# Modulation chunks of the latent attention: column tiles of 32, five chunks together in each pair of heads, one turn for all

## The chip, the cores and the metric

The kernel runs on one core of a Trainium2 chip, as one launch. The metric is the device time of that launch in microseconds (us), the median of several runs; less is better. The engines are TensorE (PE in the rows; PEld is its weight load), VectorE (DVE), ScalarE (ACT), GpSimd (POOL), and SyncE (SP), whose queue here only issues transfers.

## What is computed

One step of a two-layer diffusion model on 128 prompt tokens and 512 sample tokens, in float32. Each layer has a mixer (layer 0: latent attention; layer 1: retention) and a mixture of experts, and both are modulated by vectors that come from a condition:

```python
def modulation(cond, w, b):
    m = jax.nn.silu(cond) @ w + b
    return jnp.split(m, 6, axis=-1)
...
mod_c = modulation(cond_ctx, ada_w[layer], ada_b[layer])
mod_l = modulation(c, ada_w[layer], ada_b[layer])
hc = modulate(xc, norm1_g[layer], mod_c[0], mod_c[1])
...
oc, ctx_kv = mla_context(hc, ...)          # layer 0: 8 heads, keys and values from a latent
ol = mla_latent(hl, cache_mla[:, j], ...)  # 512 queries over 512 + 128 keys
xc = xc + mod_c[2][:, None, :] * oc
```

There are two conditions (one for the prompt, one for the sample), so each modulation is a product of 2 rows of 1024 with a matrix of 1024 x 6144, for two layers: 24 chunks of 512 columns in all.

## The kernel before

**Stages.** `setup` transposes the input and makes `silu_cond`, the two conditions after silu as [128, 8, 2]. Then, for layer 0, `mla_project` (norm, down-projections), `mla_pairs` (attention, four pairs of heads in a loop), the experts; then layer 1. The change touches `setup`, `mla_project` and `mla_pairs`. Engines meet at the end of each stage's block; within a block each engine runs its own list of instructions, and waits on semaphores that the others raise. The order in each list is written out by hand.

**Chunks.** A chunk of `ada_w` is [1024, 512], 2 MB, in one of the slots of a ring of weights. `ada_chunk` multiplies it as the moving operand: eight products over k, with the two columns of `silu_cond` as weights. Product k writes to partitions 32*(k%4) and the one after it, so four stand side by side in the array's columns, at partitions 0, 32, 64 and 96 of one PSUM bank. Each float32 product is two matmuls in the trace. The result is 2 useful rows in each of four groups. DVE copies the bank to SBUF (`take_rows`, L876 in the pairs, L532 in `mla_project`), PE turns it (`ada_turn`, L283: four products with `pick`, which adds the four groups and leaves 2 columns each), and DVE adds the bias into `modulation` (L882, L541). Four chunks (`FIRST`) are done in `mla_project`, five (`PER_PAIR`) in each of the four pairs.

**A pair of heads.** In the order of PE's list: q (three products), keys, S0 and S1, values v0 to v2, then ten units u, one for each of 2 heads x 5 tiles of 128 queries. S(u) are the scores of unit u (L706 and L707; over 640 keys, but over 128 for u = 0 and 5). DVE takes their maximum (L901, L899), ACT the exponential, DVE divides (L859), PE transposes (T(u), L716), and ACT and DVE copy the transposed tile out (L814, L865). PE issues S(u+2) ahead of T(u). After T8 and T9 come O0 and O1, the products with the values, and then w0 to w7, the output projection (L801). The chunks A0 to A4 and their turns B0 to B2 stand between these: A0, A1 ahead of S2; B0 after T1; A2 ahead of T4; B1 after T5; A3 ahead of T8; A4 after O1; B2 ahead of w2. Bank n of a product is given by its place in the list `order` modulo 4, and the helper `free` makes PE wait for whoever empties what stood four places earlier.

**DVE's list** in unit u: maximum of S(u), then the division for u-1, then the copy of T(u-1), then what `TAKE_AT` and `BIAS_AT` ask for. So a copy of a chunk's rows stands ahead of the maximum of the next unit.

**Transfers.** SP loads the next pair's chunk x into its slot once the product `A{x}` of this pair is done.

Of the kernel before, what the change touches and what calls it, by code (L numbers as in the profile page):

```python
# [20 lines left out]
P = 128  # L21
D = 1024
KD = D // P
# [51 lines left out]
BASE_COLS = {"ident": P, "ones": P, "before": P, "iota16": NE, "iota4": NG, "iotab": NBLK, "pick": 2}  # L75
# [17 lines left out]
def shape_constants():  # L93
# [5 lines left out]
            one * np.arange(NBLK), p % 32 == np.arange(2)]  # L99
# [64 lines left out]
def setup(c, cond):  # L164

    nc, ops, ps = c.nc, c.ops, c.ps
    with ExitStack() as st:
# [7 lines left out]
        with nc.Block(no_gpsimd_drain=True) as block:  # L175
# [15 lines left out]
            @block.gpsimd  # L191
            def _(pool):
                pool.memset(c.eps[:, :], EPS).then_inc(memsets, 1)
                pool.memset(rows_b[:, :], 0.0).then_inc(memsets, 1)

            @block.scalar
            def _(act):
# [3 lines left out]
                act.wait_ge(memsets, 2)  # L201
# [14 lines left out]
                for j in range(2):  # L216
                    nc.scalar.activation(cond[:, :, j], c.cols_b[:, 8 * j:8 * j + 8], ACT.Silu).then_inc(silued, 1)

            @block.tensor
            def _(pe):  # L220
                pe.wait_ge(consts_in, 16)
                pe.wait_ge(rows_in, 16 * 7)
                pe.wait_ge(memsets, 2)
# [162 lines left out]
def mla_project(c, m, j, call, amp, shift):  # L386
# [5 lines left out]
    with ExitStack() as st:  # L392
# [6 lines left out]
        ada_rows = sq[:, :, :].rearrange("p b n -> p (b n)")[:, 0:FIRST * 512].rearrange("p (x n) -> p x n", x=FIRST)  # L399
        cleared, ada_used, ada_rowed, ada_turned, biased = sems(  # L400
            nc, st, "ada", ["cleared", "used", "rows", "turned", "biased"])
# [13 lines left out]
        with nc.Block(no_gpsimd_drain=True) as block:  # L415
# [22 lines left out]
            def _(pe):  # L438
                def first_chunk(n):
                    pe.wait_ge(c.ada_first[n], 16)  # L440
                    ada_chunk(c, pe, n, (0, 3, 4, 5)[n]).then_inc(ada_used, 1)

                def first_turn(n):
                    pe.wait_ge(ada_rowed, n + 1)
                    ada_turn(c, pe, ps[:, 4, 8 * n:8 * n + 8], ada_rows[:, n, :]).then_inc(ada_turned, 1)

                pe.wait_ge(cleared, 1)
# [5 lines left out]
                for n in range(FIRST):  # L453
                    first_turn(n)
# [74 lines left out]
            def _(dve):  # L529
                def take_rows(n):  # L530
                    dve.wait_ge(ada_used, n + 1)
                    dve.tensor_copy(ada_rows[:, n, :], ps[:, n, :]).then_inc(ada_rowed, 1)  # L532
# [8 lines left out]
                dve.tensor_tensor(c.mod[:, 0, 0:16, :], ps[:, 4, 0:32].rearrange("p (m j) -> p m j", j=2),  # L541
                                  c.cols_a[:, 32:48].unsqueeze(2).to_broadcast([P, 16, 2]), ALU.add).then_inc(biased, 1)
# [64 lines left out]
def mla_pairs(c, m, layer, j):  # L607
# [5 lines left out]
    TURNS = ((0, 1), (2,), (3, 4))  # L613
    ADA_AT, TURN_AT, TAKE_AT, BIAS_AT = {4: 2, 8: 3}, {1: 0, 5: 1}, {1: (0, 1), 4: (2,), 8: (3,)}, {3: 0, 6: 1}
    order = ["q0", "q1", "qp", "k0", "qs", "k1", "S0", "S1", "v0", "v1", "v2", "A0", "A1"]
    for u in range(NU):
        order += ([f"S{u + 2}"] if u + 2 < NU else []) + ([f"A{ADA_AT[u]}"] if u in ADA_AT else []) + [f"T{u}"]
        order += ([f"B{TURN_AT[u]}"] if u in TURN_AT else []) + (["O0"] if u == NU - 2 else [])
    order += ["O1", "A4"] + [f"w{d}" for d in range(KD)]
# [1534 lines left out]
```

## Time and profile before

| | |
|---|---|
| time, median of 3 runs | 2346.25 us (2345.98 to 2348.88) |
| the profiled execution | 2346.19 us |
| its span, first to last instruction | 2344.5 us |
| PE busy | 2086.2 us, 89% of the span |
| DVE busy | 1151.9 us, 49% |
| ACT busy | 897.7 us, 38% |
| mean granted clock of TensorE | 0.908 of full |

The profiled execution took 1.69 us more than its span. The share of an engine is the union of its instructions' times; PE's 89% is no measure of how well it is used, since the four products of a chunk that run side by side count once. The row PEclk gives the clock that TensorE was granted in tenths of 2.4 GHz; the chip knows two levels, 2.4 and 1.2 GHz. A digit between 5 and 9 is a mean over a slice in which both occurred.

### The profile page before, as it was taken

Reading aid. Unit: us, or ns where it says so; the run is one execution under the profiler, and the core shown is the slowest. Engines: PE = TensorE matmul, PEld = TensorE weight load, DVE = VectorE, ACT = ScalarE, POOL = GpSimd, SP = SyncE. Lnnn points to the kernel's source line nnn. Section 1 sums busy time; section 2 is a strip of 40 time slices with the busy share of each in tenths; the row PEclk is TensorE's granted clock in tenths of the full one; section 3 lists DMA queues with packets and bytes.
Section 4 is the critical chain, followed back from the end, with each engine's and each line's share of the span. In section 5 each row is a group of like instructions: output and inputs, shape, how many; then the busy total and the mean of one; then the engine's idle time right before and its main releaser. Section 6 shows DMA issues by size and latency. Waiting matters only on the chain. (4 is left out here: it accounts for less than half of the span.)

```text
span 2344.5 us, 25727 instructions
## 1 busy us (share of the span) xinstructions
PE 2086.2 (89%) x8708; PEld 1439.6 (61%) x8708; DVE 1151.9 (49%) x1667; ACT 897.7 (38%) x1270; POOL 111.7 (5%) x128
## 2 busy tenths in 40 slices
PE   4988989898849999956999999999999975999995
PEld 2543545454538888746764874775587444878883
DVE  2132223232459999954423323242342245999994
ACT  2221111111338888824221222121122134888873
POOL 0000000000020000010100100010010002000001
PEclk7997969695869999966999999999999987999998
DMA  9942324210559999824220221221120057999974
GB/s 331 394 153 88 140 73 137 79 54 0 211 203 383 398 399 399 334 108 158 75 79 25 100 73 37 73 72 54 55 72 18 1 215 251 394 398 399 398 273 161
DMA packets 181470, 425.81 MB, mean 182 GB/s; under 512 B 10629, under 2 KB 22426, under 8 KB 181402
## 3 DMA queue, kind: packets, MB, share of 16 engines
q1 hardware_dynamic: 165056, 366.04, 42.8%
q0 software_dynamic: 10944, 39.85, 4.5%
q10 hardware_dynamic: 5402, 18.95, 2.0%
q8 instruction: 50, 0.82, 0.1%
q14 instruction: 18, 0.15, 0.0%
HBM read 369.61 MB, written 55.21 MB: 181 GB/s over the span
## 5 line engine op out<-in xcount | busy, mean ns | idle before, releaser
L1873 DVE TENSOR_TENSOR moe_w_lo<-weight_ring,moe_w_hi 128x1024 fp32r<-128x1024 f32 x432 | 520.6, 1222 | 84.7 <-ACT moe_w_hi L1804 69.2
L1804 ACT ACTIVATE moe_w_hi<-weight_ring 128x1024 fp32r<-128x1024 f32 x432 | 456.8, 1062 | 193.8 <-PE ps L1736 125.0
L1736 PE MATMUL ps<-moe_w_hi,moe_rows_t_hi 128*128 128x512 f32 x576 | 233.1, 405 | 5.1 <-DVE moe_rows_t_lo L1878 4.7
L1323 DVE TENSOR_TENSOR ret_w_lo<-weight_ring,ret_w_hi 128x512 fp32r<-128x512 f32 x128 | 95.9, 749 | 283.8 <-ACT ret_w_hi L1258 283.8
L1736 PE MATMUL ps<-moe_w_hi,moe_rows_t_lo 128*128 128x512 f32 x576 | 226.7, 394 | 0.0
L1736 PE MATMUL ps<-moe_w_lo,moe_rows_t_hi 128*128 128x512 f32 x576 | 226.3, 393 | 0.0
L1258 ACT ACTIVATE ret_w_hi<-weight_ring 128x512 fp32r<-128x512 f32 x128 | 80.6, 633 | 309.5 <-PE ps L1131 309.5
L1131 PE MATMUL ps<-ret_w_hi,h_hi 128*128 128x512 f32 x480 | 194.0, 404 | 3.4 <-ACT weight_ring L1262 2.1
L1131 PE MATMUL ps<-ret_w_hi,h_lo 128*128 128x512 f32 x480 | 189.6, 395 | 0.0
L1131 PE MATMUL ps<-ret_w_lo,h_hi 128*128 128x512 f32 x480 | 189.5, 395 | 0.0
L1736 PEld LDWEIGHTS ps<-moe_w_hi,moe_rows_t_hi 128*128 128x128 f32 x576 | 109.5, 190 | 27.2 <-DVE moe_rows_t_lo L1878 5.5
L1736 PEld LDWEIGHTS ps<-moe_w_hi,moe_rows_t_lo 128*128 128x128 f32 x576 | 109.2, 190 | 23.9
L1736 PEld LDWEIGHTS ps<-moe_w_lo,moe_rows_t_hi 128*128 128x128 f32 x576 | 109.6, 190 | 20.9
L1736 PE MATMUL ps<-moe_w_hi,moe_hidden_t_hi 128*128 128x512 f32 x288 | 114.6, 398 | 3.0 <-DVE moe_hidden_t_lo L1883 3.0
L1736 PE MATMUL ps<-moe_w_hi,moe_hidden_t_lo 128*128 128x512 f32 x288 | 113.8, 395 | 0.0
L1242 PE MATMUL ps<-weight_ring 128*128 128x512 f32 x256 | 110.9, 594 | 3.2 <-ACT weight_ring L1309 3.2
L1736 PE MATMUL ps<-moe_w_lo,moe_hidden_t_hi 128*128 128x512 f32 x288 | 113.8, 395 | 0.0
L1131 PEld LDWEIGHTS ps<-ret_w_hi,h_hi 128*128 128x128 f32 x480 | 90.0, 187 | 29.1 <-ACT weight_ring L1262 3.2
L1131 PEld LDWEIGHTS ps<-ret_w_lo,h_hi 128*128 128x128 f32 x480 | 90.0, 188 | 23.1 <-issue 1.9
L1131 PEld LDWEIGHTS ps<-ret_w_hi,h_lo 128*128 128x128 f32 x480 | 90.0, 187 | 22.0
L1217 PE MATMUL ps<-weight_ring 128*128 128x512 f32 x224 | 99.8, 594 | 2.2 <-DVE weight_ring L1334 2.2
L1131 PE MATMUL ps<-h_hi,ret_w_hi 128*128 128x320 f32 x256 | 80.9, 316 | 19.6 <-DVE ret_w_lo L1323 19.6
(304 smaller groups left out, 2990.2 us busy)
## 6 DMA issues: line engine op xcount, KB each, us to landing
weight_ring<-in_moe_w_gate SPq DMA_DIRECT2D x36, 2048.0 KB, 13.2
weight_ring<-in_moe_w_up SPq DMA_DIRECT2D x36, 2048.0 KB, 14.2
weight_ring<-in_moe_w_down SPq DMA_DIRECT2D x36, 2048.0 KB, 13.3
weight_ring<-in_ada_w SPq DMA_DIRECT2D x24, 2048.0 KB, 9.8
weight_ring<-in_ret_w_in SPq DMA_DIRECT2D x12, 2048.0 KB, 8.7
h_normed<-rows_in POOLq DMA_DIRECT2D x36, 512.0 KB, 7.1
rows_out<-h_normed ACTq DMA_DIRECT2D x36, 512.0 KB, 6.2
rows_in<-zero_rows SPq DMA_DIRECT2D x26, 512.0 KB, 13.9
```

The source lines that it names most:

```text
L1131: mm = pe.matmul(out, lhs, rhs, start=(k == 0 and x == 0), stop=(k == KD - 1 and x == 2))
L1217: mm = pe.matmul(out, lhs, rhs, start=(x == 0), stop=(x == len(mms) - 1))
L1242: mm = pe.matmul(ps[:, bank(f"w{d}"), :], wo[:, b, d * P:(d + 1) * P], yt[:, b, SEQ:T], start=(b == 0), stop=(b == 3))
L1258: nc.scalar.activation(whi[:, n % BUF, :], win[s][:, k, :], ACT.Identity).then_inc(w_hi, 1)
L1323: dve.tensor_tensor(wlo[:, n % BUF, :], win[s][:, k, :], whi[:, n % BUF, :].bitcast(F32), ALU.subtract).then_inc(w_lo, 1)
L1736: mm = pe.matmul(out, lhs, rhs, start=(first and x == 0), stop=(last and x == 2))
L1804: nc.scalar.activation(whi[:, x, :], part(u, w + x), ACT.Identity).then_inc(w_hi, 1)
L1873: dve.tensor_tensor(wlo[:, x, :], part(blk[1], w + x), whi[:, x, :].bitcast(F32), ALU.subtract).then_inc(w_lo, 1)
```

## The change

The weights of a chunk's product are now 32 columns wide instead of 2, and the conditions stand in them at an offset that depends on the chunk. `silu_cond` is [128, 8, 40]: zeros but for columns 8 and 9. Chunk number `at` takes columns 8-2at to 40-2at, so its two rows fall on rows 2at and 2at+1 of each group of 32, and all chunks of a set accumulate in one bank; the other rows get zeros added. One copy to SBUF and one turn of four products then serve the set; `pick` is 32 columns wide, of which the first 2*chunks are used. In `mla_project` the memset of four banks, which DVE made so that unwritten rows were zero, is gone. In the pairs all five chunks stand after T4, their turn after T5, the copy on DVE in unit 5 and the bias in unit 6, and SP waits once for all five before it loads the next five.

```diff
-            one * np.arange(NBLK), p % 32 == np.arange(2)]
+            one * np.arange(NBLK), p % 32 == np.arange(32)]
...
+                pool.memset(cond[:, :, :], 0.0).then_inc(memsets, 1)
...
-                    nc.scalar.activation(cond[:, :, j], c.cols_b[:, 8 * j:8 * j + 8], ACT.Silu).then_inc(silued, 1)
+                    nc.scalar.activation(cond[:, :, 8 + j], c.cols_b[:, 8 * j:8 * j + 8], ACT.Silu).then_inc(silued, 1)
...
-def ada_chunk(c, pe, bank, slot):
+def ada_chunk(c, pe, bank, slot, at, chunks):
...
-        mm = pe.matmul(c.ps[g:g + 2, bank, :], c.cond[:, k, :], w[:, k, :], start=(k < 4), stop=(k >= 4))
+        mm = pe.matmul(c.ps[g:g + 32, bank, :], c.cond[:, k, 8 - 2 * at:40 - 2 * at], w[:, k, :], start=(at == 0 and k < 4),
+                       stop=(at == chunks - 1 and k >= 4))
...
-def ada_turn(c, pe, out, rows):
+def ada_turn(c, pe, out, rows, chunks):
     for b in range(4):
-        mm = pe.matmul(out[:, 2 * b:2 * b + 2], rows[:, b * P:(b + 1) * P], c.base["pick"], start=True, stop=True)
+        mm = pe.matmul(out[:, b * 2 * chunks:(b + 1) * 2 * chunks], rows[:, b * P:(b + 1) * P], c.base["pick"][:, 0:2 * chunks],
+                       start=True, stop=True)
...
+def ada_bias(c, dve, at, turned, chunks):
+
+    n = 4 * chunks
+    return dve.tensor_tensor(c.mod[:, :, :, :].rearrange("p l m j -> p (l m) j")[:, bass.ds(at, n), :]
+                             .rearrange("p (x b) j -> p b x j", b=4),
+                             turned[:, 0:2 * n].rearrange("p (b x j) -> p b x j", b=4, j=2),
+                             c.cols_a[:, bass.ds(at + 32, n)].rearrange("p (x b) -> p b x", b=4).unsqueeze(3)
+                             .to_broadcast([P, 4, chunks, 2]), ALU.add)
...
-                pe.wait_ge(cleared, 1)
                 first_chunk(0)
                 first_chunk(1)
                 normed.tensor(pe)
                 first_chunk(2)
                 first_chunk(3)
-                for n in range(FIRST):
-                    first_turn(n)
+                pe.wait_ge(ada_rowed, 1)
+                ada_turn(c, pe, ps[:, 4, :], ada_rows, FIRST).then_inc(ada_turned, 1)
...
-                dve.memset(ps[:, 0:4, :], 0.0).then_inc(cleared, 1)
-                take_rows(0)
-                take_rows(1)
                 normed.vector_roots(dve)
-                take_rows(2)
-                take_rows(3)
-                dve.wait_ge(ada_turned, FIRST)
...
+                dve.wait_ge(ada_used, FIRST)
+                dve.tensor_copy(ada_rows, ps[:, 0, :]).then_inc(ada_rowed, 1)
+                dve.wait_ge(ada_turned, 1)
+                ada_bias(c, dve, 0, ps[:, 4, :], FIRST).then_inc(biased, 1)
...
+                    sp.wait_ge(prod.sem, prod.value("ada", i))
                     for x in range(PER_PAIR):
-                        sp.wait_ge(prod.sem, prod.value(f"A{x}", i))
                         load_ada_pair(c, sp, i + 1, x)
...
+                        if u == 5:
+                            dve.wait_ge(prod.sem, prod.value("ada", i))
+                            dve.tensor_copy(ada_rows, ps[:, bank["ada"], :]).then_inc(dve_s, 1)
+                        if u == 6:
+                            dve.wait_ge(ada_turned, i + 1)
+                            ada_bias(c, dve, i * (4 * PER_PAIR) + 4 * FIRST, ps[:, bank["ada"] + 1, :], PER_PAIR).then_inc(dve_s, 1)
```

The order on PE after the values, before (L706, L707: scores; L716: transposes; L277: chunk; L283: turn). It begins with the last of the values and ends with B0:

```order
L775 MATMUL ps<-mla_w_ukv,mla_ckv 128x256 x4
...
L277 MATMUL ps<-weight_ring,silu_cond 2x512 x8
...
L706 MATMUL ps<-mla_k,mla_q 128x320
L707 MATMUL ps<-mla_kpe,mla_qpe 128x320
...
L716 MATMUL ps<-base_consts,mla_prob 128x128 x5
L696 REGISTER_ALU
L283 MATMUL ps<-base_consts,mla_qrope 128x2 x8
```

After the change the same place (L769 is the values, L704 and L705 the scores, L714 the transposes) reads:

```order
L769 MATMUL ps<-mla_w_ukv,mla_ckv 128x256 x4
L694 REGISTER_ALU
L704 MATMUL ps<-mla_k,mla_q 128x320
L705 MATMUL ps<-mla_kpe,mla_qpe 128x320
...
L714 MATMUL ps<-base_consts,mla_prob 128x128 x5
L694 REGISTER_ALU
L704 MATMUL ps<-mla_k,mla_q 128x320
```

A0, A1 and B0 are gone from here: S2 follows v2, and S4 follows T1.

On PE from T4 to T6 after the change, where the chunks (L279) and the turn (L286) now stand:

```order
L714 MATMUL ps<-base_consts,mla_prob 128x128 x5
L694 REGISTER_ALU
L279 MATMUL ps<-weight_ring,silu_cond 32x512 x40
...
L704 MATMUL ps<-mla_k,mla_q 128x320
...
L714 MATMUL ps<-base_consts,mla_prob 128x128
L779 REGISTER_ALU
L286 MATMUL ps<-base_consts,mla_qrope 128x10 x4
```

All forty products of the five chunks stand in one piece between T4 and S7, and four turning products after T5 take the place of twenty in three places.

On DVE at the end of the units, before (L865: copy of T7; L876: rows of A3; L901, L903, L857, L859: maximum, scaled maximum, reciprocal and division for T8):

```order
L865 COPY h_normed<-ps 128x128
L873 REGISTER_ALU
L876 COPY mla_qrope<-ps 128x512
L897 REGISTER_ALU
L901 TENSOR_REDUCE mla_max<-ps 128x1
L902 REGISTER_ALU
L903 TENSOR_SCALAR mla_bias<-mla_max 128x1
L856 REGISTER_ALU
L857 RECIPROCAL mla_inv<-mla_den 128x1
L858 REGISTER_ALU
L859 TENSOR_SCALAR mla_prob<-mla_prob,mla_inv 128x640
```

and after (L855, L876, L878, L847, L849 are the same steps):

```order
L855 COPY h_normed<-ps 128x128
L872 REGISTER_ALU
L876 TENSOR_REDUCE mla_max<-ps 128x1
L877 REGISTER_ALU
L878 TENSOR_SCALAR mla_bias<-mla_max 128x1
L846 REGISTER_ALU
L847 RECIPROCAL mla_inv<-mla_den 128x1
L848 REGISTER_ALU
L849 TENSOR_SCALAR mla_prob<-mla_prob,mla_inv 128x640
```

The copy of chunk rows, which waited for A3, no longer stands between T7 and T8; one such copy stands in unit 5.

## Rows read from the trace of the kernel before

**Rows 1.** The page: PE's share, and granted clock in 40 slices.

```profile
PE 2086.2 (89%) x8708; PEld 1439.6 (61%) x8708; DVE 1151.9 (49%) x1667; ACT 897.7 (38%) x1270; POOL 111.7 (5%) x128
...
PEclk7997969695869999966999999999999987999998
```

**Rows 2.** Timeline of PE, first row of three pairs: start us, us, what.

```profile
133.90 12.41 PE L681 MATMUL ps<-mla_cq,weight_ring 128*128 128x128 f32 x36 [4.26 <-DVEq L887]
...
370.63 9.90 PE L681 MATMUL ps<-mla_cq,weight_ring 128*128 128x128 f32 x36
...
490.00 9.90 PE L681 MATMUL ps<-mla_cq,weight_ring 128*128 128x128 f32 x36
```

**Rows 3.** Timeline of PE in the second pair; in brackets idle time before, releaser.

```profile
251.28 9.90 PE L681 MATMUL ps<-mla_cq,weight_ring 128*128 128x128 f32 x36
...
277.23 3.62 PE L277 MATMUL ps<-weight_ring,silu_cond 128*2 128x512 f32 x32
280.78 0.81 PE L706 MATMUL ps<-mla_k,mla_q 128*128 128x320 f32 x2
...
286.71 0.76 PE L716 MATMUL ps<-base_consts,mla_prob 128*128 128x128 f32 x5
287.31 1.86 PE L283 MATMUL ps<-base_consts,mla_qrope 128*128 128x2 f32 x16
...
295.59 0.63 PE L706 MATMUL ps<-mla_k,mla_q 128*128 128x128 f32 x2
...
298.04 1.33 PE L716 MATMUL ps<-base_consts,mla_prob 128*128 128x128 f32 x5 [1.09 <-DVE mla_prob L859]
299.16 1.27 PE L706 MATMUL ps<-mla_k,mla_q 128*128 128x320 f32 x2
...
304.45 3.59 PE L277 MATMUL ps<-weight_ring,silu_cond 128*2 128x512 f32 x16
...
331.30 2.91 PE L277 MATMUL ps<-weight_ring,silu_cond 128*2 128x512 f32 x16
336.64 1.23 PE L716 MATMUL ps<-base_consts,mla_prob 128*128 128x128 f32 x5 [2.44 <-DVE mla_prob L859]
...
349.61 1.90 PE L277 MATMUL ps<-weight_ring,silu_cond 128*2 128x512 f32 x16
351.44 4.59 PE L801 MATMUL ps<-mla_o,weight_ring 128*128 128x128 f32 x16
```

**Rows 4.** Busy time by stretch (PE, PEld, DVE, ACT, POOL), granted clock, DMA share, GB/s.

```profile
251.30:289.00 37.70, 36.81 (x161) 20.35 (x160) 9.34 (x22) 8.84 (x20) 0.00 (x0) 1.00 0.38 132
289.00:333.40 44.40, 41.41 (x108) 18.41 (x111) 9.90 (x29) 7.84 (x18) 0.00 (x0) 0.50 0.22 78
...
176.40:179.80 3.40, 2.07 (x12) 1.32 (x11) 1.81 (x6) 1.01 (x2) 0.00 (x0) 1.00 0.41 153
179.80:190.00 10.20, 9.91 (x29) 3.36 (x29) 0.52 (x2) 1.04 (x3) 0.00 (x0) 0.50 0.01 2
```

**Rows 5.** Timeline of the first chunks in `mla_project`, PE and DVE.

```profile
34.22 6.38 PE L277 MATMUL ps<-weight_ring,silu_cond 128*2 128x512 f32 x32 [15.25 <-DVE ps L534]
42.15 7.73 PE L330 MATMUL ps<-base_consts,h_normed 128*128 128x1 f32 x40 [1.56 <-DVE h_normed L347]
...
32.40 1.76 DVE L534 MEMSET ps<- 128x2048 f32 x1 [13.14 <-PEq L175]
...
58.98 0.69 DVE L532 COPY mla_squares<-ps 128x512 f32<-128x512 f32 x1 [1.02 <-PE ps L277]
62.61 0.19 DVE L541 TENSOR_TENSOR modulation<-ps,norm_gain_and_ada_bias 128x32 f32<-128x32 f32 x1 [2.93 <-PE ps L283]
```

**Rows 6.** Weight loads by form, 120 to 640 us: chunk (2 columns), router (16).

```profile
L277 PEld LDWEIGHTS ps<-weight_ring,silu_cond 128*2 128x2 f32 x320 | 7.5, 93 | 30.8 <-issue 29.4 <-ACT mla_prob L843 1.3
L1557 PEld LDWEIGHTS ps<-h_normed,router_w 128*16 128x16 f32 x32 | 3.0, 98 | 7.9 <-ACT h_normed L322 4.7 <-issue 3.0
```

**Rows 7.** The page: transfers, KB each, median us from issue to landing.

```profile
weight_ring<-in_ada_w SPq DMA_DIRECT2D x24, 2048.0 KB, 9.8
```

More of the change, by code:

```diff
@@ L71, in before @@
         return i * self.per + self.ahead
-BASE_COLS = {"ident": P, "ones": P, "before": P, "iota16": NE, "iota4": NG, "iotab": NBLK, "pick": 2}
+BASE_COLS = {"ident": P, "ones": P, "before": P, "iota16": NE, "iota4": NG, "iotab": NBLK, "pick": 32}
 MLA_COLS = {"swap": P, "rcos": LAT, "rsin": LAT}
@@ L398, in mla_project @@
         rope = st.enter_context(nc.sbuf_tensor("mla_rope_parts", [P, 2, LAT], F32))
[L399 to L401 removed]
+        ada_rows = sq[:, 0, 0:512]
+        ada_used, ada_rowed, ada_turned, biased = sems(
+            nc, st, "ada", ["used", "rows", "turned", "biased"])
         loaded = c.w_in_full
@@ L630, in mla_pairs @@
         dve_names += [f"t{u - 1}"] if u and UNITS[u - 1][1] else []
-        dve_names += [f"ar{x}" for x in TAKE_AT.get(u, ())] + ([f"bm{BIAS_AT[u]}"] if u in BIAS_AT else [])
-    dve_names += [f"i{NU - 1}", f"p{NU - 1}", f"t{NU - 1}", "o00", "o01", "o10", "o11", "ar4"] + [f"x{d}{r}" for d in range(KD) for r in range(2)]
-    dve_names.insert(dve_names.index("x20"), "bm2")
+        dve_names += ["ar"] if u == 5 else ["bias"] if u == 6 else []
+    dve_names += [f"i{NU - 1}", f"p{NU - 1}", f"t{NU - 1}", "o00", "o01", "o10", "o11"] + [f"x{d}{r}" for d in range(KD) for r in range(2)]
     last = {"q0": ("a", "q01"), "q1": ("a", "q11"), "qp": ("a", "qp1"), "qs": ("v", "rs"), "k0": ("a", "k0"), "k1": ("a", "k1"),
@@ L638, in mla_pairs @@
     last |= {f"w{d}": ("v", f"x{d}1") for d in range(KD)}
-    last |= {f"A{x}": ("v", f"ar{x}") for x in range(PER_PAIR)} | {f"B{y}": ("v", f"bm{y}") for y in range(len(TURNS))}
+    last |= {"ada": ("v", "bias")}
     with ExitStack() as st:
@@ L654, in mla_pairs @@
         fq, fkv, fo = c.wq_full, c.wkv_full, c.wo_full
-        done, act_s, dve_s = sems(nc, st, "mla", ["products", "act", "dve"])
+        done, act_s, dve_s, ada_turned = sems(nc, st, "mla", ["products", "act", "dve", "ada_turned"])
         prod = Steps(done, order)
-        act_n, dve_n = Steps(act_s, act_names, 1), Steps(dve_s, dve_names, 5)
+        act_n, dve_n = Steps(act_s, act_names, 1), Steps(dve_s, dve_names, 7)
         by = {"a": act_n, "v": dve_n}
@@ L729, in attend, with ada @@
                     mm.then_inc(done, 1)
-                def ada(x, i):
-                    free(f"A{x}", i)
-                    pe.wait_ge(c.ada_full[x], (i + 1) * 16)
-                    ada_chunk(c, pe, bank[f"A{x}"], 1 + x).then_inc(done, 1)
-                def ada_turns(y, i):
-                    free(f"B{y}", i)
-                    for at, x in enumerate(TURNS[y]):
-                        pe.wait_ge(dve_n.sem, dve_n.value(f"ar{x}", i))
-                        mm = ada_turn(c, pe, ps[:, bank[f"B{y}"], 8 * at:8 * at + 8], ada_rows[:, x % 2, :])
+                def ada(i):
+                    free("ada", i)
+                    for x in range(PER_PAIR):
+                        pe.wait_ge(c.ada_full[x], (i + 1) * 16)
+                        mm = ada_chunk(c, pe, bank["ada"], 1 + x, x, PER_PAIR)
                     mm.then_inc(done, 1)
@@ L759, in keys @@
                         mm.then_inc(done, 1)
+                    pe.wait_ge(dve_n.sem, dve_n.before(i))
                     keys(0)
@@ L2108, in trunk_step @@
                 with ExitStack() as st:
-                    c.cond = st.enter_context(nc.sbuf_tensor("silu_cond", [P, KD, 2], F32))
+                    c.cond = st.enter_context(nc.sbuf_tensor("silu_cond", [P, KD, 40], F32))
                     c.wkv = st.enter_context(nc.sbuf_tensor("mla_w_ukv", [P, 2 * 512], F32))
```

73 lines of the change are left out of this document (19 added, 54 removed).

## The prediction

> **What bounds the kernel now.** Read the page first: PE is busy 89% of the span, and its granted clock falls to 6 or 7 tenths in every second slice between 176 and 586 us, the four pairs of heads [rows 1]. Then the timeline of PE by pair: the pairs begin at 133.90, 251.28, 370.63 and 490.00 us, so the first takes 117.4 and the next two 119.35 and 119.37 us [rows 2, 3]. I take the second as the pattern; the fourth runs the same list. Inside it PE has nearly no gaps (36.81 busy of 37.70 us, then 41.41 of 44.40 [rows 4]); the waits that end last are for DVE's division, 1.09 us before T3 and 2.44 us before T8 [rows 3]. So the path is PE's list plus a few waits on DVE, and an edit to that list counts in full.
>
> The stretches show a second thing: the clock is 1.00 from 251.3 to 289.0 and 0.50 from 289.0 to 333.4 [rows 4]. A unit of scores (four pairs of L706 and L707) takes about 2.9 us before 289 (S2, T0 and S3 together 280.78 to 286.71, 5.93 us) and 5.29 us at 299.16 [rows 3]. The clock fell as B0 ended, 16 small products of 2 columns each (from 287.31, 1.86 us [rows 3]). It came back at 333.4, 2.1 us into A3 (331.30), but not after A2 alone at 304.45. In the first pair it fell at 179.8, after 3.4 us in which PE was busy for 2.07 [rows 4], the stretch with S5 and the wait before T3; so that wait alone can bring it down.
>
> **Part by part, one pair (second, 119.35 us).** Differences of starts in [rows 3].
>
> 1. *q to v2*: unchanged, 251.28 to 277.23: 25.95.
> 2. *A0, A1*: leave this place (3.55 us for two, 1.78 each at 2.4 GHz). S2, T0, S3 stay, 5.93. T0 has been waiting: its division needs nothing that the chunks covered.
> 3. *T1* 0.60 (286.71 to 287.31). *B0* is gone, about 1.7.
> 4. *S4* 2.9, *T2* 0.6: at 2.4 GHz now, since B0, ahead of the fall, is gone.
> 5. *S5 and the wait for T3*: 2.45 (295.59 to 298.04), set by DVE, the same at either clock.
> 6. *T3, S6, T4*: at 1.2 GHz 1.12 + 5.29 + 1.12 = 7.5, at 2.4 GHz 0.6 + 2.9 + 0.6 = 4.1. The wait before T3 stays and brings the clock down during S6, I take in its middle: 0.6 + 4.1 + 1.12 = 5.8.
> 7. *Five chunks*. 3.59 us each at 1.2 GHz, 1.78 at 2.4. The row that A3 gives (back after 2.1 us) and the one that A2 gives (not back in 3.59) bound the low part; I take 4.5 us, one chunk and a quarter: 4.5 + 3.75 x 1.78 = 11.2. DVE stands still behind its wait for them, with the maximum of S6 and the divisions for T5 and T6 behind it. After it come a 0.69 us copy [rows 5], a maximum and a division, which S7 (2.9) covers; if S7 were shorter than about 2.7, T5 would be late, and then the turn.
> 8. *S7, T5, S8* 5.93 like S2, T0, S3; *the turn*, four products instead of eight, 1.73/2 = 0.9; *T6, S9, T7* 0.6 + 2.9 + 0.6. Together 10.9.
> 9. *Wait before T8*. Before, A3 and its row copy on DVE stood there: 331.30 to 336.64, 5.34. Now only DVE's chain remains, the same steps as between T2 and T3: 2.45.
> 10. *T8, O0, T9, O1*: left as they are, 336.64 to 349.61: 12.97.
> 11. *A4* (1.83) is gone from between O1 and w0. It hid DVE's copy of O1's two ranges (0.69 for the wide one, about 1.0 for both), which w1's second half waits for: 0.5 stays visible.
> 12. *w0 to w7*: 351.44 to 370.63 less B2: 19.19 - 1.7 = 17.5.
>
> Sum: 25.95 + 5.93 + 0.6 + 3.5 + 2.45 + 5.8 + 11.2 + 10.9 + 2.45 + 12.97 + 0.5 + 17.5 = 99.8 us. A pair saves 119.35 - 99.8 = 19.6, three of them 58.7. The first begins at a low clock (q takes 12.41 against 9.90 [rows 2]): 99.8 + 2.5 = 102.3, against 117.4, saves 15.1.
>
> *mla_project*: PE stood until 34.22 for DVE's memset (32.40, 1.76 us [rows 5]), now it starts 1.8 us earlier. The first two chunks take 6.4 us at either start, and L330 began only at 42.15, 1.5 us after them, since DVE had copied their rows ahead of the norm's sums; without these copies the sums lie under the chunks, so L330 starts at 32.4 + 6.4 = 38.8 and not 42.15: 3.35 saved. From the last chunk to `modulation` it was about 3.7 us (62.61 less 58.98, where the last copy starts); now a copy 0.69, a turn 0.9, and hand-overs, 1.8: 1.9 saved. Together 5.2.
>
> *At no cost*: the memset of `silu_cond` on POOL (ACT issues other transfers meanwhile); 30 more columns of constants; the transfers of the next five chunks, which SP now issues together half a pair ahead of use: 5 x 9.8 = 49 us at worst [rows 7], against some 100 from one pair's chunks to the next's. If that cover went, PE would stand in front of the chunks. The four PSUM places are spread anew; each product's predecessor four places earlier is emptied well before, except T5, which waits for the exponential of S6, done some 2.7 us after the chunks, still inside S7.
>
> *Wider weights*. No row shows a 32-column load side by side with others. 2 columns take 93 ns, 16 take 98 [rows 6], so 32 stay near 0.1 us, and four products share one 0.43 us step (1.78 us in 16 matmuls, four abreast). Below: nothing. Above: if the loads came one after another and uncovered, 16 x 0.1 = 1.6 us a chunk, 38 for 24 chunks. I take nothing, since the row of 16 is the nearest.
>
> The Trainium skill speaks to this point. "TensorE: Matmul & The Clock Gate", in its section on packing small matmuls, gives three column tiles of 32 a measured speed of 2.38 times, not 3. By that the overlap here would be about four fifths, an estimate of 0.4 us a chunk or 9 us in all, and the time would be 2276. The trace has 1.78 us a chunk against 16 x 0.43 = 6.8 if nothing overlapped, 3.8 times for four, with 2-column weights; no run here shows 32.
>
> **The sum.** 58.7 + 15.1 + 5.2 = 79.0. The profiled execution took 2346.19 us (span 2344.5 and 1.7 around it), the median is 2346.25, so nothing is to be corrected: **2267 us**. All after the last pair moves up unchanged.
>
> **Rivals.**
> - *The clock stays up in all of a pair.* For it: with B0 gone, the only low stretch left before the chunks is the wait before T3, and where the fall comes depends on how the stretches lie. Against: 179.8 us in the first pair [rows 4], where that wait sufficed. Then step 6 is 4.1 and step 7 8.9: 95.8 a pair; 3 x 23.6 + 19.1 + 5.2 = 95: 2251.
> - *The clock stays down* from T3 to T8. For it: scores alone didn't bring it back in 289.0 to 333.4. Against: five chunks in one piece are longer than A3. Then step 6 is 7.5, step 7 18.0, step 8 19.2 (scores 5.29 each): about 116.6; 3 x 2.75 - 1.7 + 5.2 = 12: 2334. A part of it, coming back after the chunks' first half, gives 2285 to 2300.
> - *The wide loads show*: up to 38 us, 2267 to 2305.
> - *Slower: four tiles of 32 columns don't run side by side.* A chunk then costs 16 x 0.43 = 6.8 us, 5.05 more, times 24 = 121: 2267 + 121 = 2388. It decides against the change from 79/24 = 3.3 us more a chunk, that is 5.1 us. For it: nothing in the trace uses full 32-column tiles. Against: the outputs already lie at 0, 32, 64 and 96, and the rows show four abreast.
> - *The change does little*: a new wait eats the gain. PE's list has no room for 79 us of it; only transfers could (five at once), and they have twice the time.
>
> **Chances.** Forecast (2255 to 2280) 0.68; clock up throughout 0.10; clock down for longer 0.12, a third of it above 2300; loads that show 0.04; little effect 0.01; no overlap 0.05. About 0.2% (4.7 us) is what a measurement of this kernel tells from no change. Faster 0.94, same 0.01, slower 0.05. The range goes from the clock's upper bound with some room, 2245, to 2300: it leaves out no overlap and the worst of the low clock.
>
> **What the profile after would show.** Steps 2 to 4: S4 in about 2.9 us in every pair, clock 1.00 up to T3. Step 7: forty products in one piece, 9 to 12 us, 1.78 a chunk once the clock is up; more than 2.2 at 1.00 says that wide tiles cost. Step 9: 2.4 us between T7 and T8 less the transposes. Step 11: 0.5 idle before w0's second half. Pairs 98 to 102 us apart. `mla_project`: first chunk at 32.4, `modulation` near 57.4. Wrong it would be if the clock fell at another place, above all among S7 to S9 after the chunks, where the turn of small products stands, or if T5 waited.

## The result and the profile after

The changed kernel takes 2251.62 us (median of 4 runs, 2249.09 to 2252.78), the kernel before 2346.11 (4 runs, 2335.98 to 2348.88). The ratio is 0.9603, 95% interval 0.9573 to 0.9633: 94.5 us less, where 79 were forecast (2267 us, range 2245 to 2300). The profiled execution took 2252.78 us, with a span of 2251.1.

The page of the changed kernel first: PE's share and the granted clock in 40 slices. They answer to [rows 1].

```profile
PE 2005.7 (89%) x8556; PEld 1402.9 (62%) x8556; DVE 1136.1 (50%) x1639; ACT 897.1 (40%) x1270; POOL 112.0 (5%) x129
...
PEclk8989999987799999769999999999999968999998
```

The slices of the pairs (3rd to 9th) now read 8 to 9; before, every second one read 5 to 7 (the last of them 5, where the prediction says 6 or 7). Then the timeline of PE, the first row of the first and of the third pair (start us, us, what):

```profile
122.41 12.10 PE L679 MATMUL ps<-mla_cq,weight_ring 128*128 128x128 f32 x36 [4.61 <-DVEq L862]
...
320.86 9.90 PE L679 MATMUL ps<-mla_cq,weight_ring 128*128 128x128 f32 x36
```

The pairs start at 122.41, 221.94, 320.86 and 416.53 and the last ends at 515.59: 99.5, 98.9, 95.7 and 99.1 us, where before they took 117.4, 119.35, 119.37 and 119.5. So 82.4 us come from the pairs and 11.5 from what is ahead of them (122.41 against 133.90). After them nothing changed: 1735.5 us to the end of the span, 1735.0 before. (These are differences within the two profiles, whose spans differ by 93.4 us; the medians differ by 94.5.)

Inside the second pair, from T1 on (the same timeline, answering to [rows 3]):

```profile
253.64 0.76 PE L714 MATMUL ps<-base_consts,mla_prob 128*128 128x128 f32 x5
...
257.07 0.77 PE L714 MATMUL ps<-base_consts,mla_prob 128*128 128x128 f32 x5
257.68 0.39 PE L704 MATMUL ps<-mla_k,mla_q 128*128 128x128 f32 x2
...
259.84 1.33 PE L714 MATMUL ps<-base_consts,mla_prob 128*128 128x128 f32 x5 [1.36 <-DVE mla_prob L849]
...
267.51 10.04 PE L279 MATMUL ps<-weight_ring,silu_cond 128*32 128x512 f32 x80
277.48 0.81 PE L704 MATMUL ps<-mla_k,mla_q 128*128 128x320 f32 x2
...
280.59 0.96 PE L286 MATMUL ps<-base_consts,mla_qrope 128*128 128x10 f32 x8
...
290.52 1.32 PE L714 MATMUL ps<-base_consts,mla_prob 128*128 128x128 f32 x5 [2.00 <-DVE mla_prob L849]
...
303.38 17.64 PE L791 MATMUL ps<-mla_o,weight_ring 128*128 128x128 f32 x64
```

The five chunks are one piece of 80 matmul records (two per product), and before w0 (L791) there is no idle time at all. The windows of that stretch (busy time of PE, PEld, DVE, ACT, POOL; granted clock; DMA share; GB/s), which answer to [rows 4]:

```profile
253.60:259.80 6.20, 4.88 (x23) 2.78 (x22) 3.68 (x10) 2.73 (x5) 0.00 (x0) 1.00 0.00 0
259.80:270.00 10.20, 10.16 (x30) 4.49 (x34) 1.59 (x6) 1.83 (x6) 0.00 (x0) 0.50 0.00 0
270.00:290.60 20.60, 18.60 (x116) 7.55 (x109) 7.40 (x20) 4.89 (x11) 0.00 (x0) 1.00 0.60 215
290.60:294.00 3.40, 3.40 (x10) 2.37 (x11) 0.91 (x3) 0.67 (x2) 0.00 (x0) 0.50 1.05 386
294.00:320.90 26.90, 26.15 (x90) 13.67 (x90) 9.04 (x19) 1.87 (x2) 0.00 (x0) 1.00 0.48 177
```

The reader is to see that the clock is at half speed for 10.2 and 3.4 us of this pair, both times from the end of a wait on DVE's division. Before it was 44.4 and 3.4. Over the four pairs the stretches at half speed add up to 182.4 us before and 48.7 after. How much a microsecond of them is worth can be read inside the changed kernel: its third pair has 6.8 us less of them than its second and is 3.25 us shorter, 0.48 each. The same comparison of two pairs gives 0.47 and 0.46 in the profiles of two runs below (the memset back, another order of k), so I take 0.47. By this estimate 133.7 us less of low clock are about 63 of the 82.4 us. The other 19.6, or 4.9 a pair, are work and waits that are gone: the turns (40 records a pair in three pieces before, 1.86 us for 16 of them [rows 3], and 8 records in 0.96 us now) and some waits on DVE. Before, a pair had three of these, 1.09, 1.90 and 2.44 us; now it has two, 1.36 and 2.00. The prediction doesn't name the middle one, before T4:

```profile
309.94 1.33 PE L716 MATMUL ps<-base_consts,mla_prob 128*128 128x128 f32 x5 [1.90 <-DVE mla_prob L859]
```

### The profile page after: what moved, and what is told of

Same layout as the page of the kernel before. It is cut to its first block and busy times, and to the rows that moved or that the text cites. A ratio compares the mean times of both kernels' runs of the same rounds, so it can differ in the third digit from the quotient of the medians.

```text
span 2251.1 us, 25291 instructions
## 1 busy us (share of the span) xinstructions
PE 2005.7 (89%) x8556; PEld 1402.9 (62%) x8556; DVE 1136.1 (50%) x1639; ACT 897.1 (40%) x1270; POOL 112.0 (5%) x129
## 5 line engine op out<-in xcount | busy, mean ns | idle before, releaser
L1296 DVE TENSOR_TENSOR ret_w_lo<-weight_ring,ret_w_hi 128x512 fp32r<-128x512 f32 x128 | 95.8, 749 | 282.4 <-ACT ret_w_hi L1231 282.4
L1190 PE MATMUL ps<-weight_ring 128*128 128x512 f32 x224 | 99.8, 594 | 2.2 <-DVE weight_ring L1307 2.2
L1104 PE MATMUL ps<-h_hi,ret_w_hi 128*128 128x320 f32 x256 | 80.2, 313 | 19.6 <-DVE ret_w_lo L1296 19.6
## 6 DMA issues: line engine op xcount, KB each, us to landing
weight_ring<-in_moe_w_down SPq DMA_DIRECT2D x36, 2048.0 KB, 12.9
weight_ring<-in_ada_w SPq DMA_DIRECT2D x24, 2048.0 KB, 15.9
```

The costliest lines, as they stand in the source:

```text
L1104: mm = pe.matmul(out, lhs, rhs, start=(k == 0 and x == 0), stop=(k == KD - 1 and x == 2))
L1190: mm = pe.matmul(out, lhs, rhs, start=(x == 0), stop=(x == len(mms) - 1))
L1296: dve.tensor_tensor(wlo[:, n % BUF, :], win[s][:, k, :], whi[:, n % BUF, :].bitcast(F32), ALU.subtract).then_inc(w_lo, 1)
```

## The experiments

The kernel before was timed again beside these: 2348.16 us (13 runs, 2333.11 to 2352.09), 2346.77 us (11 runs, 2333.41 to 2351.63) and 2348.08 us (17 runs, 2335.10 to 2351.83), one for each group of kernels. Differences to the changed kernel are against its 2251.6 us. What follows the last pair takes between 1735.0 and 1740.8 us in the eleven profiles, though no edit reaches it; a difference of under 5 us in the whole time is therefore read only where the profile shows its place.

**Wide chunks alone.** The kernel before with 32 columns a product, for which the conditions are padded with zeros, and nothing else. Here and below only the lines that matter are shown.

```
-        mm = pe.matmul(c.ps[g:g + 2, bank, :], c.cond[:, k, :], w[:, k, :], start=(k < 4), stop=(k >= 4))
+        mm = pe.matmul(c.ps[g:g + 32, bank, :], c.cond[:, k, 8:40], w[:, k, :], start=(k < 4), stop=(k >= 4))
```

> The kernel before, with nothing changed but the width of the chunk weights: 32 columns instead of 2 (columns 8 to 40 of the padded conditions, each chunk in its own bank as before, order and turns as before, the memset kept). If the gain of the change comes from the new places and the single turn (my theory), width alone does nothing: 2346 us within 5, a chunk pair still 3.55 us, weight loads about 0.11 us instead of 0.09, still under the products. If 32-column tiles by themselves helped (rival: they keep the clock up, or share the array better), this kernel would already be tens of us faster. If they cost something that the change hides, it would be slower, up to 38 us.

Measured: 2348.33 us, ratio 1.0014 (0.9991 to 1.0037). The pairs take 117.5, 119.4, 119.5 and 119.6 us, as before, and the low stretches add up to 182.5 us (182.4 before). So the width gives nothing and costs nothing. The rival with up to 38 us for wide loads falls, and so does the one with 5 us a chunk.

**The memset back.** The changed kernel waits again for a memset of four PSUM banks on DVE before the first chunk.

```
+                pe.wait_ge(cleared, 1)
                 first_chunk(0)
...
+                dve.memset(ps[:, 0:4, :], 0.0).then_inc(cleared, 1)
...
                 dve.wait_ge(ada_used, FIRST)
```

> The changed kernel with DVE's memset of four banks back in front of the first chunk of the projection stage, PE waiting for it. The prediction had 1.8 us for it. The trace of the changed kernel gained 11.5 us ahead of the first pair, where the prediction had 5.2; the surplus stands where the second chunk and the norm's sums ran at the high clock. Theory: the memset costs its 2.5 us (start 34.2 instead of 31.7) and, where it shifts the chunks against the clock's rise and fall, a few us more: 2253 to 2258. Rival: the whole surplus of 6 us hangs on it: 2260.

Measured: 2259.27 us, ratio 0.9619 (0.9603 to 0.9635), 7.7 more than the changed kernel. In the profile the first chunk starts at 34.16 instead of 31.69 and the first pair at 125.78 instead of 122.41, so 3.4 us stand in the stage itself. The pairs together take 390.0 us (393.2 without the memset) and what follows them 1737.8 (1735.5). But the profiled execution is the fastest of the four, 2255.36 us; the others took 2258.3 to 2260.5. In two of its pairs the clock came back after 3.4 us at T3, where the profile of the changed kernel has one such pair. So the place of the rest of the 7.7 isn't shown. The time lies above the 2253 to 2258 expected and at the rival's 2260, that the whole surplus hangs on the memset, and the 3.4 us that the profile shows don't bear that rival out.

**A turn behind T1.** The changed kernel with eight small products of 2 columns, whose result nobody reads, where B0 stood.

```
                         turn(u, i)
+                        if u == 1:
+                            for y in range(8):
+                                pe.matmul(ps[:, bank["T0"] + 1, 2 * y:2 * y + 2], c.base["ones"], c.base["pick"][:, 0:2], start=True, stop=True)
```

> The changed kernel with eight small products added after T1 in each pair, of the size of the old turn B0 (128 x 128 weights, 2 columns moving), whose results nobody reads. Theory: the low activity of B0 brings the clock down at once, so S4, T2, T3 and S6 run at 1.2 GHz: 1.7 us of work and 3 to 5 us of clock in each pair, together 20 to 27 us: 2272 to 2279; granted clock falls right after these products in every pair. Rival (B0 costs its own time alone, the clock falls at T3's wait anyway): 4 x 1.7 = 7 us: 2259.

Measured: 2279.99 us, ratio 0.9703 (0.9687 to 0.9720), 28.4 more, for 4 x 1.7 = 6.8 us of work. Its timeline and windows in the second pair:

```profile
262.55 1.85 PE L778 MATMUL ps<-base_consts 128*128 128x2 f32 x16
264.26 0.79 PE L704 MATMUL ps<-mla_k,mla_q 128*128 128x320 f32 x2
264.97 0.80 PE L705 MATMUL ps<-mla_kpe,mla_qpe 64*128 64x320 f32 x2
265.70 1.44 PE L704 MATMUL ps<-mla_k,mla_q 128*128 128x320 f32 x2
...
279.43 10.40 PE L279 MATMUL ps<-weight_ring,silu_cond 128*32 128x512 f32 x80
```

```profile
262.00:265.70 3.70, 3.70 (x26) 2.83 (x25) 1.84 (x5) 1.47 (x3) 0.00 (x0) 0.99 0.00 0
265.70:282.80 17.10, 16.25 (x52) 7.65 (x54) 3.43 (x11) 3.10 (x7) 0.00 (x0) 0.50 0.00 0
282.80:290.00 7.20, 7.20 (x69) 2.03 (x62) 0.09 (x1) 0.00 (x0) 0.00 (x0) 1.00 0.00 0
```

PE counts as busy in every microsecond of the first window, yet the clock falls right after it, in the middle of S4, and stays down for 17.1 us, until 3.4 us into the chunks. So it does in each of the four pairs. Low stretches over the four pairs rise from 48.7 to 85.7 us: 37.0 x 0.47 = 17, and 6.8 of work, would be 24. The pairs together take 413.3 us, 20.1 more; part of the difference is the wait before T3, now 0.85 us and not 1.36. The other 8 of the 28.4 us stand outside the pairs in the profile, 3.0 ahead of them and 5.3 behind them, where the edit changed nothing; why is open. So 20 us are what this run shows for the small products. The step from small products to a fallen clock, read from the kernel before, holds with the order of work otherwise that of the changed kernel.

**B0 cut.** The kernel before with B0 down from eight products to two. This leaves out most of the turn of the first two chunks of each pair, so their modulation isn't computed.

```
-                        mm = ada_turn(c, pe, ps[:, bank[f"B{y}"], 8 * at:8 * at + 8], ada_rows[:, x % 2, :])
+                        if y == 0:
+                            mm = pe.matmul(ps[:, bank["B0"], 8 * at:8 * at + 8], ada_rows[:, x % 2, 0:P], c.base["ident"][:, 0:2].unsqueeze(1).to_broadcast([P, 4, 2]), start=True, stop=True)
+                        else:
+                            mm = ada_turn(c, pe, ps[:, bank[f"B{y}"], 8 * at:8 * at + 8], ada_rows[:, x % 2, :])
```

> The kernel before with the turn B0 of each pair cut from eight products to two of 8 columns, so that the modulation of the first two chunks of each pair is not what the reference wants. Only the stretch of the pairs is to be read, since the later routing may differ. Theory: the clock no longer falls after T1 but at the wait before T3, about 9 us later; each of pairs 2 to 4 is shorter by 1.3 us of work and 3 to 5 us of clock: 113 to 115 us instead of 119.4. Rival (clock falls there anyway): 118.

Measured: one run, 2305.64 us, 42.5 under the kernel before, of which 37.8 in the pairs, for some 1.3 us less of work a pair. But not evenly: the pairs take 119.1, 110.5, 99.2 and 109.0 us with 45.5, 27.3, 3.4 and 23.9 us at half speed, where 113 to 115 us were expected for each of the last three. In the third the clock stayed up until T8; in the first it fell soon after the wait before T3 (which ends at 177.2), as it does in the kernel before, and from there on the pair has 34.1 us at half speed, as many as before. So B0 is one of two triggers. Without it the wait before T3 can do the same, and only sometimes. The third pair has its chunks and the other turns where they were and still takes 99.2 us, as long as a pair of the changed kernel. So where the clock stays up, one piece of five chunks isn't needed for the gain; no run tries one turn with the chunks left apart.

**Another order of k.** The changed kernel with products that share a column group next to each other.

```
-    for k in range(KD):
+    for k in (0, 4, 1, 5, 2, 6, 3, 7):
```

> The changed kernel with the eight products of a chunk in the order k = 0, 4, 1, 5, 2, 6, 3, 7, so that every second one follows one of its own column group; same products, same sums, same places. Theory: four tiles of 32 columns run side by side, and a product waits only for the one before it in its own group. Then a chunk takes five steps of 0.86 us instead of two, 4.3 us instead of 1.75, and 24 chunks cost 24 x 2.5 = 61 us more: 2313. Rival (the order in the list does not matter, the array reorders or shares): 2252. Rival (they never overlapped by groups but by something else, as the pipelining of any products): 2252 too.

Measured: 2254.89 us, ratio 0.9610 (0.9582 to 0.9638): 3.3 more, where 61 were expected. By the profile the pairs take 393.2 us together, exactly as in the changed kernel; 2.8 of the difference stand behind them. That theory falls: the neighbour's group doesn't matter. The next run asks whether groups matter at all.

**One group a chunk.** All eight products of a chunk in one column group, successive chunks in successive groups.

```
-        g = 32 * (k % 4)
+        g = 32 * (at % 4)
...
```

> Changed kernel, but all eight products of one modulation chunk are put into one column group (32 columns) instead of being spread over the four groups in turn; the four groups are filled by successive chunks. Sums and order otherwise the same. The run with the order of k changed (two products of one group behind each other) cost nothing. Theory A (what lets products overlap is that NEIGHBOURS lie in different groups, and two neighbours in one group overlap anyway for some other reason): eight in a row in one group still can't overlap beyond two, so a chunk goes from 1.78 to at least 3.4 us at 2.4 GHz, about 24 x 1.7 = 40 us more, and the clock might rise earlier, so 2275 to 2300 us. Theory B (groups do decide fully, the matmul records of the last run hid it): 6.8 us a chunk, 24 x 5 = 120 us, about 2370. Theory C (the four starts close together in the trace are the way the records are made, and a product of 32 columns takes 0.21 us a pass whatever the group is): a chunk stays at 1.78 us and the time stays within 0.3% of 2252 us.

Measured: 2340.4 us, ratio to the kernel before 0.9981 (0.9963 to 0.9999), 88.8 more than the changed kernel. Column groups do decide. The chunks of the second pair (timeline), and busy time with the count of records on their line inside the full-clock part: of this kernel, then of the changed kernel, then of the one with the other order of k.

```profile
304.42 28.96 PE L279 MATMUL ps<-weight_ring,silu_cond 128*32 128x512 f32 x80
```

```profile
310.60:326.20 15.60, 15.60 (x49) 4.23 (x48) 1.00 0.00 0
```

```profile
272.00:277.00 5.00, 5.00 (x52) 1.32 (x44) 1.00 0.00 0
```

```profile
272.10:277.10 5.00, 5.00 (x52) 1.98 (x48) 1.00 0.00 0
```

49 records in 15.6 us against 52 in 5.0. A chunk of 16 records takes 5.18 us (starts of the same record of successive chunks: 310.79, 315.97, 321.15), which is 12 steps of 0.43 us and not 16, because at each change of group four records of the next chunk start beside the last four of this one. In the run before, with four records in a group and then four in the next, the trace shows four starts within 0.1 us of each other every 0.43 us, so there all four groups are at work. A look-ahead of one fixed length over the list can't give both: to find four groups there it has to reach over 12 records, and with that reach more than four would overlap here. Four records that may stand pending in each group would give both, 12 steps here and 4 there. That is a guess that fits the two traces; no run tests it. By the records a chunk costs 5.18 - 1.72 = 3.46 us more, 24 chunks 83 of the 88.8. None of my three theories had the number. It lies between A (3.4 us a chunk) and B (6.8), since four records of each chunk overlap the next one, and not none.

**The division first.** The changed kernel, on DVE the division of each unit ahead of the next unit's maximum.

```
-        dve_names += [f"m{u}", f"b{u}"] + ([f"i{u - 1}", f"p{u - 1}"] if u else [])
+        dve_names += ([f"i{u - 1}", f"p{u - 1}"] if u else []) + [f"m{u}", f"b{u}"]
...
                         b = bank[f"S{u}"]
+                        if u:
+                            normalise(u - 1, i)
                         dve.wait_ge(prod.sem, prod.value(f"S{u}", i))
```

> The changed kernel with one thing moved on DVE: in each unit the division for the unit before stands ahead of the maximum of this unit instead of behind it. Theory: the waits before T3 (1.36 us) and T8 (2.0 us) are DVE's chain copy, maximum, division, and they bring the clock down for 3 to 10 us each; with the 1.0 us of maximum behind, T3's wait falls to 0.3 and T8's to 1.0, so each pair gains 2 us of waiting and up to 4 us of clock: 8 to 24 us in all, 2228 to 2244, and the granted clock stays up at T3. Rival (waits go, the clock falls anyway): 2244. Rival (the exponential, now started later, takes the division's place as the wait): 2252.

Measured: median 2251.06 us, ratio 0.9611 (0.9573 to 0.9648), no change, with six runs from 2239.79 to 2266.34. The profiled execution (span 2241.6) has pairs of 100.9, 95.4, 92.2 and 92.3 us. Around T3 in its first pair:

```profile
165.84 0.77 PE L714 MATMUL ps<-base_consts,mla_prob 128*128 128x128 f32 x5 [0.40 <-DVE mla_prob L849]
167.68 0.81 PE L704 MATMUL ps<-mla_k,mla_q 128*128 128x320 f32 x2 [1.07 <-ACT mla_prob L833]
```

The wait of 1.36 us has become one of 0.40 for DVE and one of 1.07 for ACT, whose exponential now comes later: the wait is moved, not removed. The clock fell behind it in two of the four pairs. The runs scatter by 26 us with the clock: the mean granted clock on record is 0.942 for the two runs of 2240 and 2243 us, 0.937 for the two of 2251 and 0.931 for the two of 2265 and 2266. From 0.942 to 0.931 there are some 52 us more at half speed, at 0.47 some 25 us. So the scatter is that of the clock, which falls in some pairs and not in others; where it fell in the slower runs, and why, isn't shown. The profile is of one of the two shortest runs.

**Chunk 0 in the gap.** The changed kernel with chunk 0 ahead of T3, where PE waits, and the other four ahead of T4 instead of behind it. The turn goes to the free half of T5's bank, and DVE copies the rows ahead of T4's tile.

```
+                        if u == 3:
+                            free("ada", i)
+                            ada(i, (0,))
+                        if u == 4:
+                            ada(i, (1, 2, 3, 4))
                         turn(u, i)
-                        if u == 4:
-                            ada(i)
...
```

> The changed kernel with the first of the five chunks moved into the wait before T3 and the other four ahead of T4 instead of behind it; the bank is held from S5 on, and the turn goes to the free half of T5's bank. Theory: 1.75 us of work fills a 2.2 us hole, so PE gains 1.3 us a pair, and the clock no longer falls at T3: 2 to 4 us more in the pairs where it did. 5 to 20 us in all: 2232 to 2247. Rival (the hole is no loss because the clock is what counts and falls anyway): 2247. Rival (T3 now waits for the exponential of S4 in its bank, the gain is eaten): 2252.

Measured: 2235.74 us, ratio 0.9532 (0.9508 to 0.9556), 15.9 less than the changed kernel. The pairs take 98.7, 93.0, 92.7 and 91.5 us. The second:

```profile
259.21 1.92 PE L279 MATMUL ps<-weight_ring,silu_cond 128*32 128x512 f32 x16
261.07 0.77 PE L716 MATMUL ps<-base_consts,mla_prob 128*128 128x128 f32 x5
...
264.51 7.07 PE L279 MATMUL ps<-weight_ring,silu_cond 128*32 128x512 f32 x64
...
285.43 1.12 PE L716 MATMUL ps<-base_consts,mla_prob 128*128 128x128 f32 x5 [2.00 <-DVE mla_prob L854]
```

The wait before T3 is gone, the clock is 1.00 up to T8, and the chunks take 1.86 us (the first) and 1.75 us. The same work in another order is worth a sixth of what the whole change gave. Low stretches in the pairs fall from 48.7 to 21.6 us, some 13 us by the 0.47; the rest is PE time that was a wait.

**Both.** Chunk 0 in the gap and the division first.

> The version with chunk 0 in the wait before T3 (2235.7 us) and, on VectorE, the division of each unit ahead of the next unit's maximum (2251.1 us alone, with its profiled pairs down to 92.3 us and its runs scattered from 2240 to 2266). If the two gains add (theory: the wait before T8 falls from about 2.0 to about 1.4 us and no longer brings the clock down for 3.4 us of the next stretch): about 0.6 + 1.5 us a pair less, so 2226 to 2230 us. Rival: the division first makes the maximum of the next unit late, so the exponential on ScalarE and then PE wait instead: 2236 us or more. Second rival: the scatter of the run with the division first comes with this order and shows here too, a spread of over 15 us.

Measured: 2230.24 us (6 runs, 2228.38 to 2234.6), ratio 0.9511 (0.9486 to 0.9536), 5.5 less again and the fastest of all. The second pair:

```profile
257.17 0.76 PE L716 MATMUL ps<-base_consts,mla_prob 128*128 128x128 f32 x5 [0.46 <-ACT mla_prob L838]
...
280.57 0.77 PE L716 MATMUL ps<-base_consts,mla_prob 128*128 128x128 f32 x5 [1.04 <-DVE mla_prob L854]
```

Before T8 1.04 us are left of 2.00, and the clock doesn't fall there; before T3 ACT's 0.46 has come back. Pairs 93.0, 90.9, 90.9 and 94.4 us; the fourth has a low stretch 19 us in, of 6.8 us, that none of the other three has. The pairs together take 369.2 us, 6.7 less than with chunk 0 in the gap alone. The time is at the upper end of the 2226 to 2230 expected. The division first gives nothing in the median by itself and some 5 us here, and the scatter is gone: 6 us.

## Why the prediction was right, step by step

The direction, the place and the mechanism held: PE's list, with the clock that the small products brought down. Two sizes were off, and they make 14.8 of the missing 15.5 us. In part the 99.8 us for a pair are luck: no single pair has the clock that the forecast gave it.

*The pairs*, forecast 99.8 us for the second: measured 98.9. By steps, from the starts in the second pair: step 1 25.86 (25.95); step 2 5.84 (5.93); steps 3 and 4 4.04 (4.1); step 5 2.16 (2.45); step 6 7.67 (5.8); step 7 9.97 (11.2); steps 8 and 9 13.04 (13.35); step 10 12.86 (12.97); steps 11 and 12 17.48 (18.0).

*Step 5* was said to be set by DVE, the same at either clock. It is set by DVE, but one thing on DVE is gone that the forecast left in: before, the bias for A0 and A1 (L882) stood between the copy of T2 and the maximum:

```profile
295.84 0.29 DVE L865 COPY h_normed<-ps 128x128 f32<-128x128 f32 x1 [6.42 <-PE ps L716]
296.16 0.17 DVE L882 TENSOR_TENSOR modulation<-ps,norm_gain_and_ada_bias 128x16 f32 x1
296.28 0.82 DVE L901 TENSOR_REDUCE mla_max<-ps 128x1 f32<-128x640 f32 x1
```

Now the maximum starts 0.20 us after the copy (257.88, 258.08) and not 0.44. That is most of the 0.29 us, here and in step 9, which took the same 2.45.

*Step 6*, the clock's fall behind the wait before T3, failed in its "I take in its middle". In the second pair the clock falls right as T3 starts and S6 and T4 run at half speed throughout, 7.67, near the bound of 7.5. In the third pair the low stretch starts at the same step but ends after 3.4 us, in the middle of S6:

```profile
352.40:358.80 6.40, 5.04 (x24) 2.83 (x23) 3.67 (x10) 2.82 (x6) 0.00 (x0) 1.00 0.00 0
358.80:362.20 3.40, 3.40 (x9) 1.87 (x9) 1.30 (x5) 1.17 (x5) 0.00 (x0) 0.50 0.00 0
362.20:375.00 12.80, 12.80 (x95) 4.50 (x95) 1.88 (x5) 0.58 (x1) 0.00 (x0) 1.00 0.05 5
```

Nothing in PE's list differs between the two. And in the first pair the same wait doesn't bring the clock down at all; it stays at 1.00 until T8:

```profile
165.79 0.77 PE L714 MATMUL ps<-base_consts,mla_prob 128*128 128x128 f32 x5 [1.36 <-DVE mla_prob L849]
...
169.92 8.79 PE L279 MATMUL ps<-weight_ring,silu_cond 128*32 128x512 f32 x80
178.64 0.81 PE L704 MATMUL ps<-mla_k,mla_q 128*128 128x320 f32 x2
```

```profile
165.70:191.60 25.90, 23.89 (x141) 10.25 (x141) 9.01 (x27) 6.62 (x16) 0.00 (x0) 1.00 0.47 168
```

So steps 6 and 7 together, 17.0 forecast, are 12.85 us in the first pair (165.79 to 178.64), 17.64 in the second, 14.49 in the third (358.75 to 373.24) and 17.63 in the fourth. The forecast put one value where there are three. The first pair's is the rival "the clock stays up" in full (4.1 + 8.9 forecast), the third's its milder form. By the time alone that rival (2251 us) looks exactly right. It isn't: it had 95.8 us for each of the last three pairs, and only the third has it.

*Step 7*: 2.6 us low of 10, not 4.5; 1.74 us a chunk at full clock (8.72 for five in the third pair). *Step 9*: 2.16 us with 2.00 idle, forecast 2.45. *Step 11*: the 0.5 us before w0 isn't there. The products of w0 that need head 0 alone stand in front of those that need O1's copy, and cover it. (In the code the wait is for w0's second half; step 11 of the prediction names w1's.) *The first pair*: 99.5 against 102.3. It gains by the clock that stays up at T3, and loses by a low stretch that was in no forecast: 6.8 us from 143.79 on, in S1, where the kernel before has none. The prediction named a fall at another place as a sign of being wrong; this one is small, some 3 us in one pair, and nothing here shows its cause. All four together: 393.2 against 401.7, 8.5 of the missing 15.5; the stage ahead has 6.3.

*mla_project*, forecast 5.2 us, measured 11.5. Timeline of PE, answering to [rows 5]:

```profile
31.69 5.04 PE L279 MATMUL ps<-weight_ring,silu_cond 128*32 128x512 f32 x32 [12.08 <-PEq L175]
36.66 4.62 PE L344 MATMUL ps<-base_consts,h_normed 128*128 128x1 f32 x40
42.72 2.50 PE L350 MATMUL ps<-norm_diagonal,base_consts 128*128 128x128 f32 x4 [1.44 <-DVE norm_diagonal L365]
45.16 5.13 PE L279 MATMUL ps<-weight_ring,silu_cond 128*32 128x512 f32 x32
51.11 1.06 PE L286 MATMUL ps<-base_consts,mla_squares 128*128 128x8 f32 x8 [0.82 <-DVE mla_squares L541]
53.64 0.46 PE L478 MATMUL ps<-h_normed,weight_ring 128*128 128x128 f32 x2 [1.47 <-ACT h_normed L336]
```

The norm's sums (L344) begin at 36.66, where 38.8 was forecast: PE starts 0.7 us earlier than taken, and the two chunks take 4.97 us from start to start and not 6.4. Then the sums take 4.62 us and not 7.73, and L350 follows 6.06 us after their start instead of 9.17: 3.1 us that the forecast didn't have. From the last two chunks to the modulation it is 7.05 us against 8.86, 1.8 saved, forecast 1.9. Ahead of the sums that is 5.5 us saved, and with 3.1, 1.8 and 1.1 further on (53.64 to 122.41 is 68.8 us, before 69.9) it makes the 11.5. The error is in the term "3.35 saved", which took the durations of before at either start. Both pieces run partly at half clock, and which part depends on when they come: here the clock is low until 34.6 us and falls again at 41.4, when the sums are all but done; before, it was low until 39.8 and fell at 43.3, just after they began. The run with wide chunks alone shows how loose these durations are: nothing moved there, and its same two pieces took 5.00 and 5.94 us. So I take the 3.1 and the 1.4 as the clock's, argued from two profiles, not shown by a run that changes it alone. The memset, 1.8 in the forecast, moves the first pair by 3.4 us in its run.

*Nothing for wide weights* held, by the run of its own. The Trainium skill's figure for three column tiles ("TensorE: Matmul & The Clock Gate", packing small matmuls) would have made it 9 us, by the prediction's estimate. Here the chunks of the changed kernel keep 52 records in 5.0 us, four abreast without loss (0.43 us for four against 0.43 for one). The run with all products of a chunk in one column group shows what stands behind it: 3.0 times as long a chunk, since there four records still overlap at each change. The Trainium skill's rule of the same section, that each tile sits where its output starts in PSUM, agrees with that pair of runs.

*The rivals.* No overlap: what was said against it held, and its price per chunk (6.8 us) would be 5.2 if all products of a chunk shared a group. Clock down longer: it didn't happen here; the run with a turn behind T1 shows what brings it about, 2280 us. T5 waits, or the turn after the chunks brings the clock down: neither happened. T5 follows S7 without a wait, the turn comes right behind it (280.59, 0.96 us), and the clock stays at 1.00 from 270.0 to 290.6.

## What to carry to other kernels

Read the granted clock beside the timeline before costing an edit: here a microsecond of half clock cost 0.47 us, and what the change saved in the pairs was, by that estimate, three parts clock to one part work and waits. Small products should be few, one turn for many chunks, and long dense products are worth more where the engine would wait: moving a chunk into the wait before T3, and the others up behind it, gave 16 us more at no cost. When a step's size depends on where the clock falls, give it a value for each case and look at each repetition in the trace, since the same two steps took 12.9, 14.5 and 17.6 us in equal pairs.

## What the runs showed of the hardware

- PE can be busy all the time by the records and still lose its clock: 16 records of 2 columns in 1.85 us, with scores ahead of and behind them, and half speed 1.3 us after their end. So it went in all four pairs of the run with the turn behind T1. It isn't a rule: in the first pair of the kernel before, 16 such records (172.44, 1.84 us) were followed by 5.5 us of full clock, until the next wait (1.62 us, before T3), in which it fell. Eight records of 10 columns in one piece of 0.96 us didn't bring it down in any pair of the changed kernel.
- Scores and transposes alone, with one wait of 0.85 us among them, didn't bring the clock back in 13.7 us after the turn behind T1 had brought it down; the chunks did, 3.4 us in. After a mere wait of 1.36 us they did, within 3.4 us, in one pair of the changed kernel (358.8 to 362.2 us), not in two others, and in the first pair the wait didn't bring the clock down.
- Four column groups of 32 run four records (two make a float32 product) for the time of one (0.43 us), and the order of neighbours matters little: blocks of four records in a group cost nothing in the pairs (393.2 us both ways), blocks of 16 cost 88.8 us in all.
- A weight load of 32 columns takes 115 ns in the pairs, of 2 columns 93 [rows 6], and neither shows in the time.
